# Second output projection in two groups of row tiles, and the first panel's products in another order, in a two-block transformer kernel

## The chip, the cores and the metric

The kernel runs on one core of a Trainium2 chip. The metric is the device time of one execution in microseconds; the median of three runs is taken.

## What is computed

Two transformer blocks follow each other on x of 1024 positions by 1024 features, all in f32. The stretches that matter here are the end of each block's mixer and the way into its feed-forward part:

```python
# first block
x_new = x + g1 * _merge(o_a, o_b, on_a[l], on_b[l], w_out[l])
h2 = _modulate(_rms_norm(x_new, norm2_g[l]), sh2, sc2)
x_new = x_new + g2 * _swiglu(h2, w_gate[l], w_up[l], w_down[l])
...
# second block
m = jnp.concatenate([a, b], axis=-1) @ w_out[l]
h = h + rmsnorm(m, post_mix_g[l])
f = rmsnorm(h, pre_ff_g[l]) @ w_ff1[l]
f = jnp.square(jax.nn.relu(f)) @ w_ff2[l]
h = h + rmsnorm(f, post_ff_g[l])
```

Here rmsnorm divides a row by the root of its mean square and multiplies by a gain. `w_out` is 1024 by 1024, `w_gate` and `w_up` 1024 by 2816, `w_ff1` 1024 by 4096.

## The kernel before

**Tiles.** The 1024 positions are eight row tiles of 128 (NT = 8). An f32 product is made of three products in a rounded format: each operand is split into a high part (a copy on ScalarE, ACT) and a low part (the difference, on VectorE, DVE), and TensorE (PE) adds hi by hi, lo by hi and hi by lo in one PSUM bank. A weight panel has 256 columns (PN); its split is one 128x2048 instruction on ACT (`split_hi`, L384) and one on DVE (`split_lo`, L388). A row tile's product with a panel is 24 matmuls (L403 to L405).

**The second output projection** is `leave_pe`, `leave_act`, `leave_dve`, `leave_pool` and `leave_sp`. It runs over 4 panels, and in each over the 8 row tiles. During panel 0 PE also turns (transposes) the next row of the operand (`turn_mixed`, L2874). ACT copies each finished tile from PSUM to `q_nat` (L2911), and in the last panel squares the row that is now whole, 1024 wide, and sums it (L2915). GpSimd (POOL) makes the row's root from the sum in two small operations (L2858, L2860). DVE then scales by root and gain (L2942) and adds to the residual `x_res` (L2946): two steps. ACT squares the new row (`square_row`, L1383), POOL makes its root (`root_row`, L1387 and L1389), and DVE scales it into `ff_rows` (`scale`, L2951). PE turns rows 0 to 3 as whole rows (`turn_row`, L1397), and ACT and DVE split them (L1416, L1420).

**The up projection** is made by `seven`, once for the first block (`f1`, names with swiglu) and once for the second (`f2`, names with ff). It takes 7 block products P1 to P7 for each pair of weight blocks (index q counts the pairs) where 8 would be usual, for which half rows and weight blocks are added and subtracted beforehand: on DVE `mix_first`, `mix_second`, `mix_third` (L1435 to L1448) for rows and `weight_sum` (L1500) for weights. The weights for a product are split by `weight_hi` (ACT, L1476) and `weight_lo` (DVE, L1480). A product (L1519 to L1521) is 12 matmuls of 512 columns.

**The first pair, q = 0,** needs the late rows turned, in five groups (g = 0 to 4) of four half rows (j = 0 to 3): `turn_block` on PE (L1411), then `block_hi` on ACT (L1424) and `block_lo` on DVE (L1428). `blocks_pe`, `blocks_act` and `blocks_dve` write the order of this stretch out by hand, the same for both blocks. On PE it is P1, P2, groups 0, 1 and 2, then P6, group 3, P5, group 4, P7, P3, P4. In the first block the same stretch follows its own output projection (`merge_*`), which already runs in 8 groups of 4 tiles (`OUT_PART`, `OUT_COL`, with columns 1 and 0 loaded twice) and interleaves the rows' additions (L2092), `modulate` (L2101, L2104) and row squares. Every engine does its own list in the order written; semaphores hold it where it needs another.

## Time and profile before

| | |
|---|---|
| three runs | 2496.49, 2500.88, 2500.69 us, median 2500.69 us |
| the profiled execution | 2507.9 us, its span 2505.7 us |
| mean granted clock of PE | 0.977 of full speed |
| PE busy, of the span | 2392.7 us, 95% |
| DVE busy | 1567.3 us, 63% |
| ACT busy | 1036.3 us, 41% |
| POOL busy | 258.0 us, 10% |

The span runs from the first to the last recorded instruction; what lies around it is 2.2 us in this execution. Busy shares are averages over stages that have different limits: PE's 5% of idle time lies in a few places, two of which are the stretches that the change touches. The profiled execution is 7 us above the median of the three runs, so differences are reckoned in the trace and laid on both.

### The profile page before, as it was taken

How to read it: one execution, taken by the hardware profiler on the slowest of the kernel's cores; microseconds unless marked ns; L12 is line 12 of the kernel's file. 1: busy time of each engine (PE TensorE's matmuls, PEld its weight loads, DVE VectorE, ACT ScalarE, POOL GpSimd, SP SyncE). 2: the span in 40 equal slices, each digit the busy share in tenths (PEclk: the TensorE clock that was granted, in tenths of full speed). 3: DMA queues.
4: the chain of work that ended last, by engine and by line, in shares of the span. 5: the costliest groups of instructions: out<-in, count | busy, mean ns of one | idle time of the engine just before them, and what ended most of it. 6: DMA issues, size and time to landing. Idle time of an engine off the chain costs nothing.

```text
span 2505.7 us, 40944 instructions
## 1 busy us (share of the span) xinstructions
PE 2392.7 (95%) x15691; PEld 2050.3 (82%) x15691; DVE 1567.3 (63%) x2612; ACT 1036.3 (41%) x1972; POOL 258.0 (10%) x253
## 2 busy tenths in 40 slices
PE   5799999999898999999999999999979999999998
PEld 2798888788797888888888898899968888788886
DVE  3632327778768777777668923234287777666677
ACT  1422226676523332332444432433255444444444
POOL 0566310000101000000000100012040000000002
PEclk8899999999998999999999999999989999999999
DMA  9233330000331232232666421110313444477553
GB/s 322 70 118 117 118 84 9 2 2 27 110 127 68 81 126 93 97 125 77 228 198 199 162 68 43 35 35 35 135 68 111 167 139 156 147 256 235 151 176 118
DMA packets 191115, 290.32 MB, mean 116 GB/s; under 512 B 11736, under 2 KB 112028, under 8 KB 190620
## 3 DMA queue, kind: packets, MB, share of 16 engines
q1 hardware_dynamic: 190940, 287.94, 34.7%
q8 instruction: 116, 1.90, 0.3%
q14 instruction: 59, 0.48, 0.1%
HBM read 221.56 MB, written 67.34 MB: 115 GB/s over the span
## 4 chain that ended last, share of the span: by engine, by line
PE 66%; DVE 3%; DMA 2%; issue 1%; POOL 1%; ACT 1%; SPq 0%; POOLq 0%; DVEq 0%; ACTq 0%
PE ps L1519 9%; PE ps L1520 9%; PE ps L1521 9%; PE ps L1761 6%; PE ps L1762 6%; PE ps L1763 6%; PE ps L403 4%; PE ps L404 4%; PE ps L405 4%; PE ps L1982 1%; PE ps L1984 1%; PE ps L1983 1%; PE ps L1411 1%; DMA stage<-w_out 0%; PE ps L2554 0%
## 5 line engine op out<-in xcount | busy, mean ns | idle before, releaser
L403 PE MATMUL ps<-w_hi,ht_hi 128*128 128x256 f32 x1488 | 435.3, 293 | 21.2 <-DVE w_lo L388 14.8
L404 PE MATMUL ps<-w_lo,ht_hi 128*128 128x256 f32 x1488 | 426.6, 287 | 0.0
L405 PE MATMUL ps<-w_hi,ht_lo 128*128 128x256 f32 x1488 | 426.3, 287 | 0.0
L403 PEld LDWEIGHTS ps<-w_hi,ht_hi 128*128 128x128 f32 x1488 | 290.9, 196 | 42.8 <-issue 20.1
L404 PEld LDWEIGHTS ps<-w_lo,ht_hi 128*128 128x128 f32 x1488 | 291.4, 196 | 0.5 <-issue 0.5
L405 PEld LDWEIGHTS ps<-w_hi,ht_lo 128*128 128x128 f32 x1488 | 291.1, 196 | 0.0
L1761 PE MATMUL ps<-ff_b_hi,ff_a_hi 128*128 128x512 f32 x448 | 174.5, 390 | 3.3 <-issue 2.1
L1763 PE MATMUL ps<-ff_b_hi,ff_a_lo 128*128 128x512 f32 x448 | 174.3, 389 | 0.0
L1762 PE MATMUL ps<-ff_b_lo,ff_a_hi 128*128 128x512 f32 x448 | 174.3, 389 | 0.0
L1519 PE MATMUL ps<-ht_hi,swiglu_w_hi 128*128 128x512 f32 x352 | 137.3, 390 | 2.4 <-DVE swiglu_gate L1558 2.4
L1722 ACT ACTIVATE ff_a_hi<-ff_a_raw 128x512 fp32r<-128x512 f32 x112 | 70.7, 631 | 165.9 <-PE ps L1763 148.8
L1520 PE MATMUL ps<-ht_lo,swiglu_w_hi 128*128 128x512 f32 x352 | 137.0, 389 | 0.0
L1521 PE MATMUL ps<-ht_hi,swiglu_w_lo 128*128 128x512 f32 x352 | 137.0, 389 | 0.0
L1476 ACT ACTIVATE swiglu_w_hi<-swiglu_stage 128x512 fp32r<-128x512 f32 x110 | 68.9, 630 | 161.7 <-PE ps L1521 153.3
L1747 DVE TENSOR_TENSOR ff_a_lo<-ff_a_raw,ff_a_hi 128x512 fp32r<-128x512 f32 x112 | 77.4, 691 | 90.0 <-ACT ff_a_hi L1722 89.8
L388 DVE TENSOR_TENSOR w_lo<-stage,w_hi 128x2048 fp32r<-128x2048 f32 x27 | 62.2, 2304 | 112.4 <-ACT w_hi L384 112.2
L1761 PE MATMUL ps<-swiglu_b_hi,swiglu_a_hi 128*128 128x512 f32 x308 | 120.7, 392 | 2.9 <-DVE swiglu_b_lo L1749 2.9
L1762 PE MATMUL ps<-swiglu_b_lo,swiglu_a_hi 128*128 128x512 f32 x308 | 120.2, 390 | 0.0
L1763 PE MATMUL ps<-swiglu_b_hi,swiglu_a_lo 128*128 128x512 f32 x308 | 120.1, 390 | 0.0
L852 ACT ACTIVATE probs<-masked,small 128x641 f32<-128x641 f32 (+3 forms) x128 | 112.0, 877 | 7.6 <-DVE small L939 5.8
L284 POOL TENSOR_SCALAR msq<-sumsq 128x1 f32<-128x1 f32 (+1 forms) x26 | 6.8, 262 | 1046.0 <-ACT junk L296 708.6
L1519 PE MATMUL ps<-ht_hi,ff_w_hi 128*128 128x512 f32 x256 | 100.8, 394 | 10.7 <-DVE ht_lo L1420 9.0
(371 smaller groups left out, 5792.0 us busy)
## 6 DMA issues: line engine op xcount, KB each, us to landing
ff_a_raw<-ff_act_dram SPq DMA_DIRECT2D x112, 256.0 KB, 2.8
stage<-w_in SPq DMA_DIRECT2D x23, 1024.0 KB, 5.3
swiglu_a_raw<-swiglu_act_dram SPq DMA_DIRECT2D x77, 256.0 KB, 2.9
stage<-w_mod SPq DMA_DIRECT2D x16, 1024.0 KB, 5.4
ff_stage<-w_ff SPq DMA_DIRECT2D x16, 1024.0 KB, 5.5
ff_act_dram<-ff_act_sums SPq DMA_DIRECT2D x16, 1024.0 KB, 4.3
ff_act_dram<-ff_acts SPq DMA_DIRECT2D x16, 768.0 KB, 5.8
swiglu_stage<-w_gate SPq DMA_DIRECT2D x11, 1024.0 KB, 6.3
```

The lines of the kernel that those rows point to most:

```text
L403: pe.matmul(bank, a, wh[:, k, :], start=(k == 0), stop=False)
L404: pe.matmul(bank, a, wl[:, k, :], start=False, stop=False)
L405: mm = pe.matmul(bank, b, wh[:, k, :], start=False, stop=(k == KT - 1))
L852: act.activation(probs_s[:, j, first:8 + CTX + width], masked_s[:, j, first:8 + CTX + width], ACT.Exp, bias=low, scale=-1.0, accum_out=den ...
L1519: pe.matmul(bank(q, b), w7_hi[b][:, k, :], x_of(0, b, k), start=(k == 0), stop=False)
L1520: pe.matmul(bank(q, b), w7_hi[b][:, k, :], x_of(1, b, k), start=False, stop=False)
L1521: mm = pe.matmul(bank(q, b), w7_lo[b][:, k, :], x_of(0, b, k), start=False, stop=(k == 3))
L1722: act.activation(a_hi[r][:, :], a_raw[s % LOOK][:, :], ACT.Copy).then_inc(f.a2_hi, 1)
L1747: dve.tensor_tensor(a_lo[r][:, :], a_raw[s % LOOK][:, :], a_hi[r][:, :].bitcast(F32), ALU.subtract).then_inc(f.a2_lo, 1)
L1761: pe.matmul(bank, a_hi[r][:, cols], b_hi[r][:, :], start=first, stop=False)
L1762: pe.matmul(bank, a_hi[r][:, cols], b_lo[r][:, :], start=False, stop=False)
L1763: return pe.matmul(bank, a_lo[r][:, cols], b_hi[r][:, :], start=False, stop=last)
```

## The change

It has two parts.

**The second output projection** takes the form of the first block's. The tiles run in 8 groups of 4 over six panel loads: rows 0 to 3 through panels 0 to 3, then rows 4 to 7 through columns 2, 3, 1 and 0; columns 1 and 0 are loaded and split a second time. ACT no longer copies a tile: it squares it straight from PSUM (`square`, after.py L2974) into a partial sum `o_sq`, 256 wide. DVE takes the tile out of PSUM with a multiplication by the gain (`evict`). POOL adds four partial sums in two small operations before the two it had (`mixed_root`). DVE adds to the residual in one step (`add`, a multiplication by the root and an addition). Whole rows 0 to 3 are turned after tiles (4, 3), (5, 0), (5, 2) and (6, 0) of the new count.

**The first pair's products** in both blocks run in the order P1, P2, P3, P5, P7, P6, P4, each placed before the last half row (or the last two) of a group; the groups have another order too (1 is now the first half of rows 0 to 3, 2 the first half and 3 the mixed second half of rows 4 to 7), and the products' PSUM banks another. P3's weights, which are made from the last weight sum, now come third on ACT and DVE. The last two `mix_first` stand inside `blocks_dve`, and the wait for the stored rows (`x1_stored`, `x3_stored`) stands behind the keeping of P1.

The diff, cut to its core:

```diff
         P1, P2, P6, P5, P7, P3, P4 = range(7)
+        FIRST = (P1, P2, P3, P5, P7, P6, P4)
...
-                    pe.wait_ge(f.mixed, f0.mixed + (8 + j + 1, 2 * j + 1, 2 * j + 2, 12 + j + 1)[g - 1])
-                pe.wait_ge(f.lo7, f0.lo7 + (3 + j // 2 if g == 0 else e + 1))
-                source = (half(4 + j, 1), half(4 + j, 1), half(j, 0), half(4 + j, 0), half(j, 1))[g]
+                    pe.wait_ge(f.mixed, f0.mixed + (2 * j + 1, 2 * j + 2, 8 + j + 1, 12 + j + 1)[g - 1])
+                held = [x for x in range(e) if late_at(x) == late_at(e)]
...
             def bank(q, b):
+                if q == 0:
+                    return ps[:, (0, 1, 7, 3, 0, 2, 4)[b], :]
                 return ps[:, (7 * q + b) % 4, :]
...
-                    pe.wait_ge(f.lo7, f0.lo7 + {P1: 4, P2: 4, P6: 12, P5: 16, P7: 20, P3: 8, P4: 24}[b])
-                if 7 * q + b >= 4:
+                    pe.wait_ge(f.lo7, f0.lo7 + {P1: 4, P2: 4, P3: 8, P5: 12, P7: 16, P6: 20, P4: 24}[b])
+                    if b == P7:
...
             f.turn_block(pe, 0, 3)
-            for g in (1, 2):
-                for j in range(4):
-                    f.turn_block(pe, g, j)
+            for j in range(3):
+                f.turn_block(pe, 1, j)
             pe.wait_ge(dense_evac, evac)
+            f.product(pe, 0, P3)
+            f.turn_block(pe, 1, 3)
+            for j in range(3):
+                f.turn_block(pe, 2, j)
+            f.product(pe, 0, P5)
+            f.turn_block(pe, 2, 3)
+            for j in range(3):
+                f.turn_block(pe, 3, j)
+            f.product(pe, 0, P7)
+            f.turn_block(pe, 3, 3)
+            f.turn_block(pe, 4, 0)
+            f.turn_block(pe, 4, 1)
             f.product(pe, 0, P6)
-            for j in range(4):
-                f.turn_block(pe, 3, j)
-            f.product(pe, 0, P5)
-            for j in range(4):
-                f.turn_block(pe, 4, j)
-            for b in (P7, P3, P4):
-                f.product(pe, 0, b)
+            f.turn_block(pe, 4, 2)
+            f.turn_block(pe, 4, 3)
+            f.product(pe, 0, P4)
             for q in range(1, f.Q):
                 for b in range(7):
                     f.product(pe, q, b)
 
-        def blocks_act(act, f):
+        def blocks_act(act, f, stored):
 
             for g in range(2):
                 for j in range(4):
                     f.block_hi(act, g, j)
-            for b in (P7, P3, P4):
+            for b in (P7, P6, P4):
                 f.weight_hi(act, 0, b)
             f.tick_act(act, 0, P1)
+            act.wait_ge(*stored)
+            for j in range(4):
+                f.block_hi(act, 2, j)
             f.tick_act(act, 0, P2)
...
+            f.mix_first(dve, 2)
             for j in range(4):
-                f.mix_second(dve, j)
                 f.block_lo(dve, 0, j)
+            f.mix_first(dve, 3)
             for j in range(4):
-                f.mix_third(dve, j)
                 f.block_lo(dve, 1, j)
-            for b in (P7, P3, P4):
-                f.weight_lo(dve, 0, b)
-            for g in (2, 3, 4):
-                for j in range(4):
-                    f.block_lo(dve, g, j)
+            f.weight_lo(dve, 0, P7)
+            for j in range(4):
+                f.block_lo(dve, 2, j)
+            f.mix_second(dve, 0)
+            f.mix_second(dve, 1)
+            f.block_lo(dve, 3, 0)
+            f.mix_second(dve, 2)
+            f.block_lo(dve, 3, 1)
+            f.mix_second(dve, 3)
+            f.block_lo(dve, 3, 2)
+            f.weight_lo(dve, 0, P6)
+            f.mix_third(dve, 0)
+            f.block_lo(dve, 3, 3)
+            f.mix_third(dve, 1)
+            f.block_lo(dve, 4, 0)
+            f.mix_third(dve, 2)
+            f.block_lo(dve, 4, 1)
+            f.mix_third(dve, 3)
+            f.weight_lo(dve, 0, P4)
+            f.block_lo(dve, 4, 2)
+            f.block_lo(dve, 4, 3)
...
-            for b in (P1, P2, P6, P5):
+            for b in (P1, P2, P3, P5):
                 f1.weight_hi(act, 0, b)
                 if b == P2:
                     square(4)
             for j in range(5, NT):
                 square(j)
             act.wait_ge(dense_done, OUT_END)
-            act.wait_ge(x1_stored, 16 * NT)
-            blocks_act(act, f1)
+            blocks_act(act, f1, (x1_stored, 16 * NT))
 
...
+            load_weights(sp, P_M + 2, panel_of(t["w_out_2"], OUT_COL[2] * PN))
             sp.wait_ge(tr_done, T_M + NT)
-            for j in range(NT):
-                sp.dma_start(x_res[:, j, :], x2_dram[j * P:(j + 1) * P, :]).then_inc(x_in[j], 16)
-            for p in range(2, 4):
-                load_weights(sp, P_M + p, panel_of(t["w_out_2"], p * PN))
+            for j in range(4):
+                x2_row(j)
+            load_weights(sp, P_M + 3, panel_of(t["w_out_2"], OUT_COL[3] * PN))
+            for j in range(4, NT):
+                x2_row(j)
+            sp.dma_start(stage_x[:, :].rearrange("p (k n) -> p k n", k=KT), panel_of(t["w_out_2"], OUT_COL[5] * PN)).then_inc(w_landed_2, 16)
...
         def leave_pool(pool):
-            for j in range(NT + 2):
-                if j < NT:
-                    pool.wait_ge(m_sq, j + 1)
-                    pool.tensor_scalar(msq[:, 8 + j:9 + j], sumsq[:, 8 + j:9 + j], 1.0 / D, EPS, ALU.mult, ALU.add).then_inc(m_ms, 1)
-                    pool.wait_ge(m_ms, j + 1)
-                    pool.tensor_tensor(rstd[:, 8 + j:9 + j], msq[:, 8 + j:9 + j], neg_half[:, 8 + j:9 + j], ALU.pow).then_inc(m_rs, 1)
-                if j >= 2:
-                    f2.root_row(pool, j - 2)
+            def mixed_root(j):
+                pool.wait_ge(m_sq, all_parts(j))
+                pool.tensor_tensor(o_ms[:, j, 0:2], o_sq[:, j, 0:2], o_sq[:, j, 2:4], ALU.add).then_inc(m_ms, 1)
+                pool.wait_ge(m_ms, 3 * j + 1)
+                pool.tensor_tensor(sumsq[:, 8 + j:9 + j], o_ms[:, j, 0:1], o_ms[:, j, 1:2], ALU.add).then_inc(m_ms, 1)
+                pool.wait_ge(m_ms, 3 * j + 2)
+                pool.tensor_scalar(msq[:, 8 + j:9 + j], sumsq[:, 8 + j:9 + j], 1.0 / D, EPS, ALU.mult, ALU.add).then_inc(m_ms, 1)
+                pool.wait_ge(m_ms, 3 * j + 3)
+                pool.tensor_tensor(rstd[:, 8 + j:9 + j], msq[:, 8 + j:9 + j], neg_half[:, 8 + j:9 + j], ALU.pow).then_inc(m_rs, 1)
+
+            for first in (0, 4):
+                mixed_root(first)
+                for j in range(first, first + 3):
+                    mixed_root(j + 1)
+                    f2.root_row(pool, j)
+                f2.root_row(pool, first + 3)
...
-            f2.turn_row(pe, 3)
+            for h in range(8):
+                for i in range(4):
+                    mixed_tile(h, i)
+                    if (h, i) in OUT_TURN:
+                        turn_mixed(OUT_TURN[h, i])
+                    if (h, i) in MIX_ROW:
+                        f2.turn_row(pe, MIX_ROW[h, i])
...
+            def added_square(j):
+                act.wait_ge(added, j + 1)
+                act.wait_ge(m_sq, (18, 19, 20, 20, 30, 31, 32, 32)[j])
+                f2.square_row(act, j, x_res[:, j, :])
...
-                        act.wait_ge(added, j - 1)
-                        act.wait_ge(m_sq, min(j + 1, NT))
-                        f2.square_row(act, j - 2, x_res[:, j - 2, :])
-                    if p == 3 and LAG_M <= j < LAG_M + 4:
-                        act.wait_ge(dense_done, D_M + 3 * NT + j - LAG_M + 1)
-                        f2.row_hi(act, j - LAG_M)
+            split(1)
+            for h in range(7):
+                for i in range(4):
+                    if (h, i) in OUT_TURN:
+                        j = OUT_TURN[h, i]
+                        turned_hi(act, j, j % 2, T_M)
+                    square(h, i)
+                    if (h, i) in MIX_SPLIT:
+                        split(MIX_SPLIT[h, i])
+                    if h == 4 and i:
+                        added_square(i - 1)
...
+            def evict(h, i):
+                x, first = OUT_PART[h]
+                j, cols = first + i, slice(OUT_COL[x] * PN, (OUT_COL[x] + 1) * PN)
+                dve.wait_ge(m_sq, 4 * h + i + 1)
...
+                    dve.wait_ge(tr_done, T_M + NT)
...
             def add(k):
                 dve.wait_ge(m_rs, k + 1)
-                dve.scalar_tensor_tensor(out=q_nat[:, k, :], in0=q_nat[:, k, :], scalar=rstd[:, 8 + k:9 + k], in1=gain_m[:, :],
-                                         op0=ALU.mult, op1=ALU.mult).then_inc(m_scaled, 1)
-                dve.wait_ge(m_scaled, k + 1)
+                dve.wait_ge(dense_evac, D_M + all_parts(k))
                 dve.wait_ge(x_in[k], 48)
-                dve.tensor_tensor(x_res[:, k, :], x_res[:, k, :], q_nat[:, k, :], ALU.add).then_inc(added, 1)
+                dve.scalar_tensor_tensor(out=x_res[:, k, :], in0=q_nat[:, k, :], scalar=rstd[:, 8 + k:9 + k], in1=x_res[:, k, :],
+                                         op0=ALU.mult, op1=ALU.add).then_inc(added, 1)
...
+            add(0)
+            evict(4, 0)
+            add(1)
+            add(2)
+            evict(4, 1)
+            add(3)
+            evict(4, 2)
+            scale(0)
+            evict(4, 3)
```

Three places of the order, each word for word. The first is POOL in the second output projection: L2858 and L2860 make the root of the projection's row, L1387 and L1389 that of the new residual row. Before, from the root of the projection's row 2 on:

```order
L2858 TENSOR_SCALAR msq<-sumsq 128x1
L2860 TENSOR_TENSOR rstd<-msq,neg_half 128x1
L1387 TENSOR_SCALAR ff_means<-ff_sums 128x1
L1389 TENSOR_TENSOR ff_roots<-ff_means,neg_half 128x1
L2858 TENSOR_SCALAR msq<-sumsq 128x1
L2860 TENSOR_TENSOR rstd<-msq,neg_half 128x1
L1387 TENSOR_SCALAR ff_means<-ff_sums 128x1
L1389 TENSOR_TENSOR ff_roots<-ff_means,neg_half 128x1
```

After, where L2913 to L2919 are `mixed_root` and L1397 and L1399 `root_row`; the fence begins with the root of row 1:

```order
L2913 TENSOR_TENSOR o_ms<-o_sq 128x2
L2915 TENSOR_TENSOR sumsq<-o_ms 128x1
L2917 TENSOR_SCALAR msq<-sumsq 128x1
L2919 TENSOR_TENSOR rstd<-msq,neg_half 128x1
L1397 TENSOR_SCALAR ff_means<-ff_sums 128x1
L1399 TENSOR_TENSOR ff_roots<-ff_means,neg_half 128x1
L2913 TENSOR_TENSOR o_ms<-o_sq 128x2
L2915 TENSOR_TENSOR sumsq<-o_ms 128x1
L2917 TENSOR_SCALAR msq<-sumsq 128x1
L2919 TENSOR_TENSOR rstd<-msq,neg_half 128x1
```

A row takes four POOL operations where it took two, and the roots of residual row 0 stand between the mixed roots of rows 1 and 2 (before, between those of rows 2 and 3).

The second place is ACT at the end of the first block's output projection: L1476 is `weight_hi`, `swiglu_stage_8608` the loaded weights, `swiglu_w_s` a weight sum, L1383 the square of a residual row. Before:

```order
L1476 ACTIVATE swiglu_w_hi_8610<-swiglu_stage_8608 128x512
L1476 ACTIVATE swiglu_w_hi_8611<-swiglu_stage_8608 128x512
L1383 ACTIVATE junk,swiglu_sums<-q_nat 128x1024
L1476 ACTIVATE swiglu_w_hi_8612<-swiglu_w_s_8625 128x512
L1476 ACTIVATE swiglu_w_hi_8613<-swiglu_w_s_8624 128x512
L1383 ACTIVATE junk,swiglu_sums<-q_nat 128x1024 x3
```

After, with L1487 for `weight_hi` and L1393 for the row square:

```order
L1487 ACTIVATE swiglu_w_hi_8610<-swiglu_stage_8608 128x512
L1487 ACTIVATE swiglu_w_hi_8611<-swiglu_stage_8608 128x512
L1393 ACTIVATE junk,swiglu_sums<-q_nat 128x1024
L1487 ACTIVATE swiglu_w_hi_8612<-swiglu_stage_8608 128x512
L1487 ACTIVATE swiglu_w_hi_8613<-swiglu_w_s_8624 128x512
L1393 ACTIVATE junk,swiglu_sums<-q_nat 128x1024 x3
```

The third weight split reads `swiglu_stage_8608` in place of the sum `swiglu_w_s_8625`; what it reads there is the block that `weight_sum` 3 writes in place, and row 5's square stands behind it.

The third place is PE in the second block's first pair, from the last matmul of P2 to the first ones of the next products: L1411 is the turning of half rows, x4 for each half row. Before:

```order
L1521 MATMUL ps<-ht_hi,ff_w_lo_8757 128x512
L1411 MATMUL ps<-ident,ff_rows 128x128 x40
L1519 MATMUL ps<-ff_t_hi_8741,ff_w_hi_8751 128x512
L1520 MATMUL ps<-ff_t_lo_8744,ff_w_hi_8751 128x512
L1521 MATMUL ps<-ff_t_hi_8741,ff_w_lo_8758 128x512
```

After, with L1422 for the turning and L1536 to L1538 for products:

```order
L1538 MATMUL ps<-ht_hi,ff_w_lo_8757 128x512
L1422 MATMUL ps<-ident,ff_rows 128x128 x20
L1536 MATMUL ps<-ht_hi,ff_w_hi_8751 128x512
L1537 MATMUL ps<-ht_lo,ff_w_hi_8751 128x512
L1538 MATMUL ps<-ht_hi,ff_w_lo_8758 128x512
```

Forty turnings, ten half rows, stood between P2 and the next product; now it is twenty, five half rows, and the next product is P3, which reads operands of group 0's kind (`ht_hi`) where P6 read those of group 1 (`ff_t_hi_8741`).

## Rows read from the trace of the kernel before

**Rows 1.** Page, part 1: busy time, share of the span, instructions

```profile
PE 2392.7 (95%) x15691; PEld 2050.3 (82%) x15691; DVE 1567.3 (63%) x2612; ACT 1036.3 (41%) x1972; POOL 258.0 (10%) x253
```

**Rows 2.** Waits of PE: line, released by; us in total, times, longest

```profile
PE ps L1519 <- DVE ht_lo L1420: 9.0, 1, 9.0
...
PE ps L1411 <- DVE ht_lo L1428: 4.2, 3, 3.3
```

**Rows 3.** Timeline of PE: start, duration, line; idle time before it in brackets

```profile
816.79 0.47 PE L1519 MATMUL ps<-ht_hi,swiglu_w_hi 128*128 128x512 f32 x1 [1.33 <-DVE swiglu_gate L1558]
...
835.95 0.39 PE L1519 MATMUL ps<-ht_hi,swiglu_w_hi 128*128 128x512 f32 x1
...
1740.88 0.36 PE L403 MATMUL ps<-w_hi,ht_hi 128*128 128x256 f32 x1 [1.76 <-DVE ht_lo L2932]
...
1744.62 0.36 PE L403 MATMUL ps<-w_hi,ht_hi 128*128 128x256 f32 x1
...
1843.96 0.28 PE L404 MATMUL ps<-w_lo,ht_hi 128*128 128x256 f32 x1
1844.08 0.28 PE L405 MATMUL ps<-w_hi,ht_lo 128*128 128x256 f32 x1
...
1862.29 0.77 PE L1519 MATMUL ps<-ht_hi,ff_w_hi 128*128 128x512 f32 x1 [8.95 <-DVE ht_lo L1420]
```

**Rows 4.** Timeline of DVE, the first panels of both blocks

```profile
781.61 1.22 DVE L2104 TENSOR_TENSOR swiglu_rows<-swiglu_rows,mod 128x1024 f32<-128x1024 f32 x1
...
800.83 2.48 DVE L1428 TENSOR_TENSOR swiglu_t_lo<-ps,swiglu_t_hi 128x512 fp32r<-128x512 f32 x4 [1.53 <-ACT swiglu_t_hi L1424]
805.31 2.48 DVE L1428 TENSOR_TENSOR swiglu_t_lo<-ps,swiglu_t_hi 128x512 fp32r<-128x512 f32 x4 [2.00 <-ACT swiglu_t_hi L1424]
...
1866.10 1.28 DVE L2951 SCALAR_TENSOR_TENSOR ff_rows<-x_res,ff_roots,gain_g 128x1024 f32<-128x1024 f32 x1
...
1885.16 2.48 DVE L1428 TENSOR_TENSOR ff_t_lo<-ps,ff_t_hi 128x512 fp32r<-128x512 f32 x4 [2.46 <-ACT ff_t_hi L1424]
1889.65 2.48 DVE L1428 TENSOR_TENSOR ff_t_lo<-ps,ff_t_hi 128x512 fp32r<-128x512 f32 x4 [2.00 <-ACT ff_t_hi L1424]
```

**Rows 5.** Groups by shape, 1740:1900 (L2088: 700:810): busy us, mean ns, idle before

```profile
L2911 ACT ACTIVATE q_nat<-ps 128x256 f32<-128x256 f32 x32 | 11.9, 382 | 36.9 <-PE ps L405 36.6
...
L1428 DVE TENSOR_TENSOR ff_t_lo<-ps,ff_t_hi 128x512 fp32r<-128x512 f32 x12 | 7.7, 683 | 4.5 <-ACT ff_t_hi L1424 4.5
...
L388 DVE TENSOR_TENSOR w_lo<-stage,w_hi 128x2048 fp32r<-128x2048 f32 x3 | 6.9, 2288 | 27.7 <-ACT w_hi L384 27.7
...
L2088 DVE TENSOR_TENSOR tmp<-ps,mod 128x256 f32<-128x256 f32 x24 | 10.1, 422 | 21.8 <-PE ps L1984 21.8
```

**Rows 6.** Timeline of all engines, 766.9 to 769.4, two rows

```profile
767.00 1.06 ACT L1383 ACTIVATE junk<-q_nat 128x1024 bf16<-128x1024 f32 x1 [0.69 <-DVE q_nat L2092]
...
769.34 0.68 DVE L1500 TENSOR_TENSOR swiglu_stage<-swiglu_stage,swiglu_w_s 128x512 f32<-128x512 f32 x1
```

**Rows 7.** Windows: length, busy of PE, PEld, DVE, ACT, POOL; granted clock, DMA

```profile
794.00:796.00 2.00, 1.85 (x9) 1.51 (x9) 2.00 (x4) 2.00 (x5) 0.00 (x0) 0.50 0.00 0
...
798.00:800.00 2.00, 2.00 (x13) 1.65 (x12) 1.29 (x3) 0.00 (x0) 0.00 (x0) 1.00 0.95 264
```

**Rows 8.** Timelines of the DMA queue and of ACT, second output projection

```profile
1763.59 3.71 SPq L2844 DMA_DIRECT2D x_res<-x_dram  x8
1768.19 16.76 SPq L235 DMA_DIRECT2D stage<-w_out  x2
...
1780.30 1.91 ACT L384 ACTIVATE w_hi<-stage 128x2048 fp32r<-128x2048 f32 x1 [10.57 <-DMA stage<-w_out]
```

**Rows 9.** Timeline of POOL, last panel of the second output projection

```profile
1823.48 0.19 POOL L2858 TENSOR_SCALAR msq<-sumsq 128x1 f32<-128x1 f32 x1 [84.72 <-ACT junk L2915]
1823.75 0.56 POOL L2860 TENSOR_TENSOR rstd<-msq,neg_half 128x1 f32<-128x1 f32 x1
...
1831.12 1.29 POOL L1387 TENSOR_SCALAR ff_means<-ff_sums 128x1 f32<-128x1 f32 x1
```

243 lines of the change are left out of this document (165 added, 78 removed).

## The prediction

> **What bounds the kernel now.** I read the page's first part for where idle time can be, then the chain of waits of PE, then the timelines of PE, DVE, ACT and POOL round the two stretches that the change touches. PE is busy 95% of 2505.7 us [rows 1], so the kernel is PE's work plus some pauses. Pauses that count here: 9.0 us at once before the second block's first product, and 4.2 us at turnings that wait for DVE's low parts [rows 2]. But PE's own pauses do not say what ends the stretch. In both first panels DVE is the slow one. Its last scaled row starts at 781.61 and ends at 782.83, and the low parts of the last half rows end at 805.31 + 2.48 = 807.79: 24.96 us. In the second block it is 1866.10 + 1.28 = 1867.38 to 1889.65 + 2.48 = 1892.13: 24.75 us [rows 4]. Only 1.53 + 2.00 us (first) and 2.46 + 2.00 us (second) of them is idle. The first product of q = 1 starts 9.0 us after DVE's last low part, at 816.79 [rows 3]. From there PE runs through. So each stretch is priced by when DVE hands over its last low part.
>
> **First block, rows.** In the new order P3's weights are split third. They read the block that weight sum 3 writes, which DVE does at 769.34 for 0.68 us, so ACT can't begin before 770.0. Before, row 5's square ran at 767.00 [rows 6]; now it is queued behind two weight splits on ACT, from about 771.1, and row 5's root on POOL, `modulate(5)` on DVE and all that DVE does after it wait for it. With a square of 1.06 us and 0.19 for reading its sum, a root of 0.82 us (0.19 + 0.08 + 0.55, [rows 9]) and DVE's own work up to there I get row 5 ready at 773.6 where DVE was free at 771.9: **+1.7**. What hides it otherwise is nothing: DVE has no pause from there to the last row. It would be 0 if DVE came later than I think, 3 at most (POOL's two operations at 1.29 each instead of 0.19 and 0.55 when DVE is in the way).
>
> **Both blocks, the first panel.** From the last scaled row, DVE has the same work in another order: 35 instructions of 128x512, at 0.60 us from one to the next (four take 2.48, one alone 0.68 [rows 4, 5], so the step is 1.80/3), 21.0 us, and 0.4 us of pauses between dependent ones: 21.4. The rest is idle. Before that was 3.5. In the new order DVE waits more often, since PE turns the last half row of every group behind a product: 1.3 us for half row (1, 3), behind P3; 2.0 for group 2, because ACT has three weight splits, the keeping of P1 and a wait ahead of it; 1.2 for group 3 behind P5; 1.65 for its last half row behind P7; 1.35 for the last two behind P6. Each comes out of laying the four lists side by side with the durations of the rows: a product is (835.95 - 816.79)/7 = 2.74 us at full clock [rows 3], four turnings 0.43 (a turning of eight is 0.86, below), a half row on ACT about as long as on DVE. Sum 7.5, so the stretch is 21.4 + 7.5 = 28.9 against 24.96 (first) and 24.75 (second): **+3.9 and +4.1**. The move of the two `mix_first` and of the wait for stored rows costs nothing by itself: they are in the 35, and the stores are long done. From below this could be -3.5 each (no idle at all, 21.4); from above +8 each (every product at half clock stands before a half row that DVE needs).
>
> **The clock.** Between 794 and 796 PE has nothing but turnings, is busy 1.85 of 2 us and is granted 0.50, the 1.2 GHz level; between 798 and 800, with products, it has 1.00 [rows 7]. In the new order products stand between turnings from the start, each while the clock is still at the lower level. P3 then takes 5.5 us in place of 2.74, P5 perhaps part of it, and DVE waits for the half row behind them. On DVE's path I put one such product and half of a second one, less the time that DVE had work in hand: **+4** in each block, between 0 and 8.
>
> **Second output projection.** PE's plain work: the first tile starts at 1740.88; a tile is 24 matmuls at 0.12 us (1843.96 to 1844.08) = 2.88, and with eight turnings 1744.62 - 1740.88 = 3.74, so eight turnings are 0.86 [rows 3]. Thirty-two tiles and ten turnings of eight (six of the operand, four rows of `ff_rows`) end at 1740.88 + 92.2 + 8.6 = 1841.7. To this come:
> - Panel 3. The eight rows of x_res were issued at 1763.59 ahead of the panels at 1768.19, and the panel's split began at 1780.30, after ACT had waited 10.57 for it [rows 8]. Now panel 3 is behind four rows and panel 2; by the same rate (5.2 MB in 16.7 us) it lands at 1777.9 and, with 1.91 on ACT [rows 8] and 2.29 on DVE [rows 5], is split at 1782.3. Tile (3, 0) would start at 1740.88 + 34.6 + 5.2 = 1780.7: **+1.6**.
> - Row 0. POOL's roots of mixed row 2 stand behind the roots of residual row 0, which wait for ACT's square of it, behind tile (4, 1) in ACT's list. So: tile (4, 1) done 1799.6, its square 0.57 (0.38 as the eviction of the same shape [rows 5] and 0.19), row square 1.25, POOL root 0.82, mixed root 1.36 (two more operations of 0.27), and the same again for row 1's root and mixed row 3, with DVE's additions of 1.28 [rows 4] and evictions of 0.42 (as L2088, [rows 5]) between. DVE has `add(2)` before tile (4, 1)'s eviction and `add(3)` before (4, 2)'s: `add(3)` ends at 1808.8, `scale(0)` at 1810.4 or so. PE reaches the turning of row 0 after tile (4, 3) at 1805.3: **+5.2**. Row 2 then waits 0.8, and the clock falls once more behind the pause, 1.4.
>
> That gives 1841.7 + 1.6 + 5.2 + 0.8 + 1.4 = 1850.7 for the end of the tiles, against 1844.2 now. It is not lost whole: of rows 4 to 7 less is left to do behind the tiles (one addition step of 1.28 where there were 1.28 and 1.22, and no square of 1024 behind a copy), so the last row is scaled 15.5 us behind the tiles in place of 1867.38 - 1844.2 = 23.2: 1866.2 against 1867.4, **-1.1**. The 9.0 us wait before the first product [rows 2, 3] goes into this. From below this part could be -8 (row 0 in time, POOL free), from above +4: POOL's small operations take 1.29 where one of DVE's is under way, as at 1831.12, in place of 0.19 [rows 9], and there are now two more for a row.
>
> **Sum.** First block 1.7 + 3.9 + 4 = 9.6, second -1.1 + 4.1 + 4 = 7.0: +16.6. The profiled execution of before is 2507.9, so 2524.5 there; on the median, 2500.69 + 16.6 = **2517**. The same layout for the kernel before ends within 0.7 us of its rows, so it is the new waits that can be wrong.
>
> **Rivals.**
> - *The clock doesn't matter.* If PE comes back to full clock with P3, the 8 and the 1.4 fall away: +7.2, 2507.9. For it: products stand closer together than before. Against it: at 794 to 796 it had stayed low through 1.85 us of work in 2. 0.16. The Trainium skill (TensorE: Matmul & The Clock Gate, Part 4: PE-mode transpose) says that a transpose doesn't count as PE being busy in the same way; by that rule products between turnings would bring the clock back sooner, which is this rival, and the trace agrees as far as the clock rose only with products.
> - *No change.* The clock is up and also row 0 is in time, because tile (4, 1)'s square is served at once and POOL isn't slowed: 7.2 - 5.2 = +2.0, 2502.7. 0.11.
> - *Faster.* DVE never waits in the two first panels, as the products' order means to have it: first block 1.7 + 21.4 - 24.96 = -1.9, second -1.1 + 21.4 - 24.75 = -4.5, together -6.4: 2494.3. What decides is DVE's idle time in a stretch: with x us in each, the sum is -6.4 + 2x, so below 3.2 us the kernel gains, and I count 7.5. For it: the new order gives DVE half rows of four groups to choose from. Against it: DVE's list is fixed, and the last half row of each group is behind a product of 2.74. 0.12.
> - *Worse.* Panel 3 comes later than the rate says (the first panels' loads share the queue) and the clock is low through three products in each block: 2517 + 9 or more. 0.05.
>
> The main case has the rest, 0.56, between 2506 and 2526 by its own bounds.
>
> **Range and chances.** 0.2%, 5 us, is about what a measurement can tell from no change, so "slower" begins at 2505.7. Slower: the main case, most of the first rival and the last, 0.71; the same 0.17; faster 0.12. The range takes in the main case, the clock rival and most of the next: 2501 to 2527.
>
> **What would show it.** PE waits some 5 us at a row's turning for `ff_rows` of the second block and 1 to 2 us for the low part of panel 3; the half-row stretch on DVE lasts 28 us or more with 7 or more idle, in five pieces; row 5's `modulate` in the first block waits for POOL; q = 1 starts in the first block at 822 to 827 where it was 816.79; the granted clock is 0.50 at P3. I am wrong if DVE's idle time stays under 3 us in the stretches, or if row 0's turning doesn't wait.

## The result and the profile after

| | before | after |
|---|---|---|
| median | 2500.78 us (4 runs, 2496.49 to 2505.99) | 2521.22 us (4 runs, 2518.58 to 2527.16) |
| ratio | | 1.0076, 95% interval 1.0055 to 1.0098 |
| profiled execution, its span | 2507.9, 2505.7 us | 2518.58, 2516.8 us |

The kernel is slower by 20.4 us. The two profiled executions lie only 10.7 us apart: the first block's output projection began at 664.05 before and at 658.84 after, in a part that the change doesn't touch. So positions are compared from a start of their own: in the first block from the first matmul of the output projection, in the second from the first tile of the projection there. The page after:

```profile
span 2516.8 us, 41059 instructions
...
PE 2393.7 (95%) x15691; PEld 2052.8 (82%) x15691; DVE 1575.2 (63%) x2638; ACT 1036.1 (41%) x1990; POOL 252.0 (10%) x269
```

PE's busy time is what it was (2392.7, [rows 1]). Its waits, answering to [rows 2]; L1536 is the first line of a product, L1422 the turning of a half row, L1407 of a whole row:

```profile
PE ps L1536 <- DVE swiglu_gate L1575: 5.9, 1, 5.9
PE ps L1422 <- DVE ff_rows L3069: 5.6, 2, 3.3
PE ps L1536 <- DVE ff_acts L1575: 5.2, 1, 5.2
...
PE ps L1407 <- DVE ff_rows L3069: 4.9, 2, 4.5
...
PE ps L2952 <- DVE w_lo L388: 1.5, 1, 1.5
```

The 9.0 us before P1 of the second block is gone, and the same time and more stands in many places: 5.9 and 5.2 us before q = 1 of each block, 4.9 at the turning of whole rows, 1.5 for panel 3. Now the timeline of PE, answering to [rows 3]:

```profile
820.44 0.76 PE L1536 MATMUL ps<-ht_hi,swiglu_w_hi 128*128 128x512 f32 x1 [5.87 <-DVE swiglu_gate L1575]
...
842.45 0.39 PE L1536 MATMUL ps<-ht_hi,swiglu_w_hi 128*128 128x512 f32 x1
...
1746.03 0.36 PE L2952 MATMUL ps<-w_hi,ht_hi 128*128 128x256 f32 x1 [1.67 <-issue]
...
1787.50 0.39 PE L2952 MATMUL ps<-w_hi,ht_hi 128*128 128x256 f32 x1 [1.52 <-DVE w_lo L388]
...
1815.29 1.97 PE L1407 MATMUL ps<-ident,ff_rows 128*128 128x128 f32 x8 [4.50 <-DVE ff_rows L3069]
...
1855.91 0.28 PE L2954 MATMUL ps<-w_hi,ht_lo 128*128 128x256 f32 x1
```

The tiles of the second projection issue from 1746.03 to 1855.91, 109.9 us (before 103.2). The seven products of q = 1 in the first block take 842.45 - 820.44 = 22.0 us where they took 835.95 - 816.79 = 19.2 [rows 3]. DVE in the first block's half-row stretch, answering to [rows 4]: the last scaled row, and the half rows before which it sat idle most.

```profile
777.41 1.22 DVE L2146 TENSOR_TENSOR swiglu_rows<-swiglu_rows,mod 128x1024 f32<-128x1024 f32 x1
...
788.39 0.69 DVE L1439 TENSOR_TENSOR ht_lo<-ps,ht_hi 128x512 fp32r<-128x512 f32 x1 [2.92 <-ACT ht_hi L1435]
...
791.45 2.56 DVE L1439 TENSOR_TENSOR swiglu_t_lo<-ps,swiglu_t_hi 128x512 fp32r<-128x512 f32 x4 [1.76 <-ACT swiglu_t_hi L1435]
...
795.98 0.69 DVE L1439 TENSOR_TENSOR swiglu_t_lo<-ps,swiglu_t_hi 128x512 fp32r<-128x512 f32 x1 [0.78 <-ACT swiglu_t_hi L1435]
...
799.10 0.69 DVE L1439 TENSOR_TENSOR swiglu_t_lo<-ps,swiglu_t_hi 128x512 fp32r<-128x512 f32 x1 [0.64 <-ACT swiglu_t_hi L1435]
...
804.31 0.69 DVE L1439 TENSOR_TENSOR swiglu_t_lo<-ps,swiglu_t_hi 128x512 fp32r<-128x512 f32 x1 [3.31 <-ACT swiglu_t_hi L1435]
...
810.16 1.29 DVE L1439 TENSOR_TENSOR swiglu_t_lo<-ps,swiglu_t_hi 128x512 fp32r<-128x512 f32 x2 [1.30 <-ACT swiglu_t_hi L1435]
```

From 777.41 + 1.22 = 778.63 to 810.16 + 1.29 = 811.45 it is 32.8 us in place of 24.96, with 10.9 us idle in place of 3.5. The same in the second block, from the last scaled row to the last half rows, with the wait behind P7 between them:

```profile
1870.03 1.28 DVE L3069 SCALAR_TENSOR_TENSOR ff_rows<-x_res,ff_roots,gain_g 128x1024 f32<-128x1024 f32 x1 [0.94 <-POOL ff_roots L1399]
...
1894.29 0.69 DVE L1439 TENSOR_TENSOR ff_t_lo<-ps,ff_t_hi 128x512 fp32r<-128x512 f32 x1 [2.35 <-ACT ff_t_hi L1435]
...
1900.13 1.29 DVE L1439 TENSOR_TENSOR ff_t_lo<-ps,ff_t_hi 128x512 fp32r<-128x512 f32 x2 [1.29 <-ACT ff_t_hi L1435]
```

That is 30.1 us (24.75), with 8.1 idle. The granted clock (window, its length, busy PE, PEld, DVE, ACT, POOL, clock, DMA), answering to [rows 7]:

```profile
784.00:786.00 2.00, 2.00 (x7) 1.52 (x7) 1.47 (x3) 0.14 (x1) 0.00 (x0) 0.61 0.00 0
786.00:788.00 2.00, 2.00 (x15) 1.74 (x13) 0.00 (x0) 0.24 (x1) 0.00 (x0) 1.00 0.00 0
800.00:802.00 2.00, 2.00 (x6) 1.59 (x5) 0.99 (x2) 0.00 (x0) 0.00 (x0) 0.50 0.00 0
822.00:824.00 2.00, 2.00 (x7) 1.51 (x6) 1.29 (x3) 0.79 (x2) 0.00 (x0) 0.50 0.00 0
1876.00:1878.00 2.00, 2.00 (x10) 1.60 (x9) 2.00 (x4) 0.00 (x0) 0.00 (x0) 1.00 0.00 0
```

In the first block P3, issued from 783.15 on, begins at the lower level and ends at full clock: the mean is 0.61 from 784 to 786 and 1.00 from 786 to 788. P7, at 800 to 802, is at 0.50, and so is P1 of q = 1 at 822 to 824. In the second block P3 is at full clock (1876 to 1878).

**Where the time went**, from such rows of both traces: in the first block, 1.3 us until the last row (from row 4's scaling at 766.88 and 761.38), 7.9 in the stretch, 2.8 in q = 1: 12.0. In the second, the last row is scaled 125.3 us after the first tile, before 126.5: -1.2; the stretch +5.4; q = 1 +2.7: 6.9. Together 18.9, inside the interval of the ratio (13.8 to 24.5 us). The two spans differ by only 11.1 us because the stretches that the change doesn't touch took 7.4 us less in the profiled execution of after, 5.2 of it ahead of the first block's output projection.

### The profile page after: what moved, and what is told of

It reads as the page before. It is cut to its first block and busy times, and to the rows that moved or that the text cites. A ratio compares the mean times of both kernels' runs of the same rounds, so it can differ in the third digit from the quotient of the medians.

```text
span 2516.8 us, 41059 instructions
## 1 busy us (share of the span) xinstructions
PE 2393.7 (95%) x15691; PEld 2052.8 (82%) x15691; DVE 1575.2 (63%) x2638; ACT 1036.1 (41%) x1990; POOL 252.0 (10%) x269
## 5 line engine op out<-in xcount | busy, mean ns | idle before, releaser
L403 PE MATMUL ps<-w_hi,ht_hi 128*128 128x256 f32 x1232 | 361.6, 293 | 17.6 <-DVE w_lo L388 14.8
L404 PE MATMUL ps<-w_lo,ht_hi 128*128 128x256 f32 x1232 | 353.6, 287 | 0.0
L405 PE MATMUL ps<-w_hi,ht_lo 128*128 128x256 f32 x1232 | 353.6, 287 | 0.0
L403 PEld LDWEIGHTS ps<-w_hi,ht_hi 128*128 128x128 f32 x1232 | 241.4, 196 | 38.8 <-issue 16.0
L404 PEld LDWEIGHTS ps<-w_lo,ht_hi 128*128 128x128 f32 x1232 | 241.8, 196 | 0.5 <-issue 0.5
L405 PEld LDWEIGHTS ps<-w_hi,ht_lo 128*128 128x128 f32 x1232 | 241.4, 196 | 0.0
L1536 PE MATMUL ps<-ht_hi,swiglu_w_hi 128*128 128x512 f32 x352 | 139.1, 395 | 6.1 <-DVE swiglu_gate L1575 5.9
L1538 PE MATMUL ps<-ht_hi,swiglu_w_lo 128*128 128x512 f32 x352 | 138.2, 393 | 0.0
L1487 ACT ACTIVATE swiglu_w_hi<-swiglu_stage 128x512 fp32r<-128x512 f32 x110 | 69.2, 630 | 166.8 <-PE ps L1538 153.7
L852 ACT ACTIVATE probs<-masked,small 128x641 f32<-128x641 f32 (+3 forms) x128 | 112.0, 877 | 7.6 <-DVE small L939 5.8
L788 PE MATMUL ps<-ident,probs 128*128 128x128 f32 (+1 forms) x720 | 106.6, 283 | 1.0 <-DVE prob_t L947 1.0
```

Source lines behind the costliest of these rows:

```text
L403: pe.matmul(bank, a, wh[:, k, :], start=(k == 0), stop=False)
L404: pe.matmul(bank, a, wl[:, k, :], start=False, stop=False)
L405: mm = pe.matmul(bank, b, wh[:, k, :], start=False, stop=(k == KT - 1))
L788: mm = pe.transpose(ps[0:rows, 4 + c // 4, (c % 4) * P:(c % 4 + 1) * P], probs[:, j, c * P:c * P + rows], ident[:, :])
L852: act.activation(probs_s[:, j, first:8 + CTX + width], masked_s[:, j, first:8 + CTX + width], ACT.Exp, bias=low, scale=-1.0, accum_out=den ...
L1536: pe.matmul(bank(q, b), w7_hi[w_at(q, b)][:, k, :], x_of(0, b, k), start=(k == 0), stop=False)
```

## Experiments

Twelve kernels. The table has each run's ratio to before on the same chip, and from its trace: *stretch*, from the end of the last scaled row to the end of the last half row's low part, and the idle time of DVE in it; *q = 1*, from its first product to the first of q = 2; *tiles*, from the first to the last matmul of the second projection; *row*, from that first tile to the end of the last scaled row. All in us.

| kernel | ratio (95%) | block 1 stretch, idle, q = 1 | tiles, row | block 2 stretch, idle, q = 1 |
|---|---|---|---|---|
| before | 1 | 25.0, 3.5, 19.2 | 103.2, 126.5 | 24.8, 4.5, 19.1 |
| after | 1.0076 (1.0055 to 1.0098) | 32.8, 10.9, 22.0 | 109.9, 125.3 | 30.1, 8.1, 21.8 |
| leave_only | 0.9994 (0.9982 to 1.0006) | 24.4, 2.9, 19.1 | 109.5, 124.9 | 25.5, 4.1, 19.1 |
| order_only | 1.0093 (1.0074 to 1.0113) | 31.9, 10.0, 21.8 | 104.1, 125.9 | 35.2, 13.0, 20.6 |
| leave_pool | 0.9973 (0.9962 to 0.9984) | 25.5, 4.1, 19.2 | 103.2, 118.6 | 24.5, 3.0, 19.1 |
| after_pool | 1.0051 (1.0034 to 1.0068) | 32.4, 10.5, 21.9 | 103.2, 118.6 | 29.9, 8.0, 21.8 |
| whole_groups | 1.0041 (1.0025 to 1.0056) | 26.1, 4.4, 21.7 | 109.5, 124.9 | 26.6, 4.9, 21.8 |
| act_group2 | 1.0089 (1.0073 to 1.0105) | 32.1, 10.2, 21.7 | 112.3, 127.7 | 30.6, 8.7, 21.9 |
| row5_first | 1.0082 (1.0065 to 1.0099) | 32.1, 10.2, 21.9 | 109.9, 125.3 | 30.1, 8.1, 21.7 |
| pool_fill | 0.9950 (0.9937 to 0.9963) | 23.9, 0.0, 19.0 | 104.9, 120.3 | 24.7, 0.8, 19.0 |
| pool_fill_sp | 0.9945 (0.9932 to 0.9958) | 25.8, 2.0, 19.0 | 101.4, 116.8 | 25.3, 1.4, 19.0 |
| new_repaired | 1.0000 (0.9991 to 1.0010) | 28.3, 6.6, 21.3 | 101.4, 116.8 | 25.1, 3.4, 21.3 |
| pause_filled | 1.0061 (1.0044 to 1.0078) | 32.4, 10.4, 19.2 | 112.0, 127.4 | 30.2, 8.2, 19.1 |
| turns_filled | 0.9932 (0.9915 to 0.9949) | 24.1, 0.4, 19.0 | 101.4, 116.8 | 24.1, 0.4, 19.0 |

### One part alone

**leave_only**: the change without its part on the first pair's order.

```diff
-            for b in (P1, P2, P3, P5):
+            for b in (P1, P2, P6, P5):
                 f2.weight_hi(act, 0, b)
...
             scale(7)
+            f2.mix_first(dve, 2)
+            f2.mix_first(dve, 3)
             blocks_dve(dve, f2)
```

> The second output projection in its new form, the first pair's products in the order of before. My theory: the projection itself neither gains nor loses. Its tiles end about 6.5 us later than before (some 1.5 us for the low part of panel 3, some 4.5 us at the turning of row 0), but the last scaled row comes about 1 us earlier relative to the first tile, and the half-row stretch on DVE is again 24 to 25 us. Time within 0.2% of before, 2496 to 2506 us; the first block as before. Rival: the pauses of PE in the projection are the loss, then this kernel keeps 6 to 10 us of the 20, and the stretch of the first block is not where it goes.

Measured 2501.65 us, ratio 0.9994: no change, as the theory had it, with the tiles 6.3 us longer and the last row 1.6 us earlier.

**order_only**: the other part alone, on the old projection (`blocks_*`, `seven` and `first_weights_*` of after, `leave_*` of before).

> The projection of before, the new order of the first pair's products in both blocks. My theory: this is the whole loss. In the first block q = 2 starts 11 to 12 us later after the first tile of its output projection than before, the half-row stretch on DVE is 32 to 33 us with some 11 us idle; in the second block the stretch is 29 to 31 us with 7 to 8 us idle. Sum 17 to 21 us over before, 2518 to 2522 us. Rival: the loss is in the projection, then this kernel is within 8 us of before.

Measured 2526.72 us, ratio 1.0093: 22.6 us, a little over the 17 to 21 expected, and the rival is out: the order is the whole loss. The second block's stretch is 35.2 us where 29 to 31 were expected, with 13.0 idle. 4.2 us of that is in a place where the changed kernel has none, ahead of group 0's half rows on DVE:

```profile
1880.53 1.29 DVE L1439 TENSOR_TENSOR ht_lo<-ps,ht_hi 128x512 fp32r<-128x512 f32 x2 [1.92 <-ACT ht_hi L1435]
1884.09 1.29 DVE L1439 TENSOR_TENSOR ht_lo<-ps,ht_hi 128x512 fp32r<-128x512 f32 x2 [2.27 <-ACT ht_hi L1435]
```

Behind the old projection's 9 us wait P1 is issued from 1873.72 on, 3.6 us ahead of the last scaled row's end, where the changed kernel has it 15.3 us ahead. It takes 5.25 us at a granted clock of 0.50, and group 0's half rows are turned behind it and behind P2. In before P1 is nearly as late, 5.1 us ahead, but there DVE has the mixing of half rows between the same low parts.

### POOL's order

**leave_pool** and **after_pool**: leave_only and the changed kernel with the roots in this order.

```diff
-            for first in (0, 4):
-                mixed_root(first)
-                for j in range(first, first + 3):
-                    mixed_root(j + 1)
-                    f2.root_row(pool, j)
-                f2.root_row(pool, first + 3)
+            for j in range(4):
+                mixed_root(j)
+            for j in range(4):
+                f2.root_row(pool, j)
+            mixed_root(4)
+            for j in range(4, 7):
+                mixed_root(j + 1)
+                f2.root_row(pool, j)
+            f2.root_row(pool, 7)
```

> As leave_only, with one further edit: GpSimd makes the roots of mixed rows 0 to 3 first and those of residual rows 0 to 3 behind them, so that mixed row 2 is not queued behind residual row 0. My theory: the 4.5 us wait of PE at the turning of row 0 goes (under 1 us stays), the tiles end 5 us earlier, the clock does not fall behind it, and the last scaled row comes with them: 5 to 8 us less than leave_only, 2493 to 2497 us. Rival: DVE's own list (additions and evictions) or ACT's squares hold row 0 just as long, then the wait stays above 3 us and the time is that of leave_only within 2 us.

> The changed kernel with that edit of GpSimd's order alone. My theory: the same 5 to 8 us less than the changed kernel, 2513 to 2516 us, the rest of the loss stays. Rival: in this kernel the last row hangs on DVE, not on the tiles, and nothing is gained.

The wait first, in the changed kernel: POOL's timeline where mixed row 2's four operations (L2913 on) stand behind the root of residual row 0 (L1397, L1399), and DVE's, where L3061 is the one-step addition, first of row 1 and then of row 2.

```profile
1806.87 0.19 POOL L1397 TENSOR_SCALAR ff_means<-ff_sums 128x1 f32<-128x1 f32 x1 [11.38 <-ACT junk L1393]
1807.15 0.55 POOL L1399 TENSOR_TENSOR ff_roots<-ff_means,neg_half 128x1 f32<-128x1 f32 x1
1807.66 0.19 POOL L2913 TENSOR_TENSOR o_ms<-o_sq 128x2 f32<-128x2 f32 x1
```

```profile
1803.04 1.28 DVE L3061 SCALAR_TENSOR_TENSOR x_res<-q_nat,rstd,x_res 128x1024 f32<-128x1024 f32 x1
1809.08 1.28 DVE L3061 SCALAR_TENSOR_TENSOR x_res<-q_nat,rstd,x_res 128x1024 f32<-128x1024 f32 x1 [4.76 <-POOL rstd L2919]
...
1813.96 1.27 DVE L3069 SCALAR_TENSOR_TENSOR ff_rows<-x_res,ff_roots,gain_g 128x1024 f32<-128x1024 f32 x1
```

POOL sat idle for 11.38 us before the root, and DVE for 4.76 us before row 2's addition; row 0's scaling (L3069) ran at 1813.96 and PE, ready for it since 1810.8, began to turn it at 1815.29. In leave_pool, PE's turning of the whole row 0 (L1397) has no wait:

```profile
1804.00 1.04 PE L1397 MATMUL ps<-ident,ff_rows 128*128 128x128 f32 x8
```

The tiles are back to 103.2 us and the last row comes at 118.6: 2496.51 us, ratio 0.9973, and 2515.24, 1.0051, for after_pool. Both as forecast; the gains over the kernels without the edit are 5 and 6 us.

### Inside the half-row stretch

**whole_groups**: the changed kernel with products behind whole groups on PE.

```diff
-            for j in range(3):
+            for j in range(4):
                 f.turn_block(pe, 1, j)
             pe.wait_ge(dense_evac, evac)
             f.product(pe, 0, P3)
-            f.turn_block(pe, 1, 3)
-            for j in range(3):
+            for j in range(4):
                 f.turn_block(pe, 2, j)
...
```

> The changed kernel with the new order of products, but on PE each product stands behind the whole of a group: four half rows of group 1, P3, group 2, P5, group 3, P7, group 4, P6, P4. My theory: DVE's idle time in the first block's half-row stretch (10.9 us in the changed kernel) is for 7.5 us that of half rows turned behind a product (2.92 behind P3, 3.31 behind P7, 1.30 behind P6). These pieces go, at most a third comes back elsewhere: 3 to 6 us idle, stretch 25.5 to 28.5 us in place of 32.8, 4 to 7 us in the first block and 3 to 5 in the second, 2509 to 2514 us. Rival: DVE waits for the banks and for its own mixing (the half rows are turned as soon as they can be), then the idle time stays above 9 us and the time within 3 us.

Measured 2512.37 us, ratio 1.0041, 8 to 9 us less than the changed kernel. DVE's timeline in the first block:

```profile
793.26 2.48 DVE L1439 TENSOR_TENSOR swiglu_t_lo<-ps,swiglu_t_hi 128x512 fp32r<-128x512 f32 x4 [1.95 <-ACT swiglu_t_hi L1435]
...
797.73 0.69 DVE L1439 TENSOR_TENSOR swiglu_t_lo<-ps,swiglu_t_hi 128x512 fp32r<-128x512 f32 x1 [0.78 <-ACT swiglu_t_hi L1435]
...
804.79 0.69 DVE L1439 TENSOR_TENSOR swiglu_t_lo<-ps,swiglu_t_hi 128x512 fp32r<-128x512 f32 x1 [1.31 <-ACT swiglu_t_hi L1435]
```

The idle time fell from 10.9 to 4.4 us and the stretch from 32.8 to 26.1, in the second block from 8.1 to 4.9 and from 30.1 to 26.6: what had cost was the half row left behind a product. In the first block P7 ran at full clock this time, so some 2 of the 6.7 us there can be the clock's. In the second it took 4.4 us, for the most part at the lower level, and the idle time fell all the same. But q = 1 still takes 21.7 us: that part of the loss has another cause.

**act_group2**: ScalarE's copies of group 2 ahead of two weight splits and of the keeping of P1 (`block_hi(act, 2, j)` behind `weight_hi(act, 0, P7)`).

> The changed kernel with ScalarE's copies of group 2 ahead of two of the three weight splits and of the keeping of P1. My theory: DVE's idle time before group 2 (1.76 us in both blocks) goes, the weight split of P6 is in time as before, 1 to 2 us less in each stretch, 2 to 4 us in all. Rival: group 2 is late on PE, behind P3 and its turnings, then nothing changes (within 1 us in the traces).

Measured 2524.81 us, ratio 1.0089, no gain. DVE's timeline:

```profile
792.47 1.88 DVE L1439 TENSOR_TENSOR swiglu_t_lo<-ps,swiglu_t_hi 128x512 fp32r<-128x512 f32 x3
796.21 0.69 DVE L1439 TENSOR_TENSOR swiglu_t_lo<-ps,swiglu_t_hi 128x512 fp32r<-128x512 f32 x1 [1.86 <-ACT swiglu_t_hi L1435]
...
799.26 0.69 DVE L1439 TENSOR_TENSOR swiglu_t_lo<-ps,swiglu_t_hi 128x512 fp32r<-128x512 f32 x1 [1.16 <-ACT swiglu_t_hi L1435]
```

Three half rows of group 2 are now taken at 792.47 without a pause, and the fourth waits 1.86 us at 796.21: it is turned behind P5, and was so in the changed kernel too. The pause had two causes in a row, and taking away the first showed the second: from the end of (1, 3)'s low part to the end of the stretch it is 22.3 us, and 22.4 in the changed kernel. So ScalarE's list did hold group 2, as the theory said, but it was not worth the 1 to 2 us. The rival's forecast, nothing gained, came true, with another product than the one it named: P5, not P3.

**row5_first**: the square of row 5 ahead of the third weight split.

```diff
             for b in (P1, P2, P3, P5):
                 f1.weight_hi(act, 0, b)
                 if b == P2:
                     square(4)
-            for j in range(5, NT):
+                    square(5)
+            for j in range(6, NT):
                 square(j)
```

> The changed kernel with the square of row 5 ahead of the third weight split in the first block on ScalarE. My theory: the last scaled row of the first block comes 1 to 1.7 us earlier relative to its projection's first tile (119.8 to 121.2 us in the runs with the new order, 117.9 to 120.2 in those with the old one), the stretch behind it is as long as it was: 1 to 2 us. Rival: P3's low part is then late and DVE waits for it in the place of the row: no difference.

Measured 2522.66 us, ratio 1.0082: no difference that the times can tell. The trace of the changed kernel shows what there was to get, on DVE:

```profile
761.38 1.28 DVE L2143 SCALAR_TENSOR_TENSOR swiglu_rows<-q_nat,swiglu_roots,mod 128x1024 f32<-128x1024 f32 x1
...
765.22 0.69 DVE L1491 TENSOR_TENSOR swiglu_w_lo<-swiglu_stage,swiglu_w_hi 128x512 fp32r<-128x512 f32 x1 [0.70 <-ACT swiglu_w_hi L1487]
...
767.74 1.28 DVE L2143 SCALAR_TENSOR_TENSOR swiglu_rows<-q_nat,swiglu_roots,mod 128x1024 f32<-128x1024 f32 x1 [0.43 <-POOL swiglu_roots L1399]
```

0.70 us is the way from sum 3 over ScalarE to P3's low part, only 0.43 us is row 5's root. In row5_first the wait for the root went and the 0.70 stayed: from row 4's scaling to the last row 16.7 us, where the changed kernel has 17.25 and before 15.95.

### The pause before q = 1, and the clock

**pause_filled**: the changed kernel with work of no use in PE's pause.

```diff
             f.product(pe, 0, P4)
+            for i in range(24):
+                pe.matmul(ps[:, 5, :], ht_hi[:, 0, 0:P], ht_hi[:, 0, 0:512], start=True, stop=True)
```

> The changed kernel with 24 more matmuls of 512 columns on PE, behind P4 of the first pair and ahead of q = 1, into a PSUM bank that nobody reads: some 5.5 us of work in a pause of 5.2 to 5.9 us. The result is not touched. My theory: PE's late pause costs nothing itself, since q = 1 starts when DVE is done; what costs is that the clock is at its lower level for some 5 us behind it. Filled, q = 1 starts within 0.5 us of where it did, at full clock, and the seven products of q = 1 take 19.1 us in place of 21.8 to 22.0: 2.7 us in each block, 5 us in all, 2514 to 2518 us. Rival: the products of q = 1 are slow since they wait for weights or for joined banks, then they take 21.8 us again, at full clock.

Measured 2520.09 us, ratio 1.0061. PE's timeline and a window of the first products of q = 1 (L1907 is the filling):

```profile
816.43 5.60 PE L1907 MATMUL ps<-ht_hi 128*128 128x512 f32 x24
822.47 0.47 PE L1536 MATMUL ps<-ht_hi,swiglu_w_hi 128*128 128x512 f32 x1 [0.44 <-DVE swiglu_gate L1575]
```

```profile
824.00:826.00 2.00, 2.00 (x11) 1.63 (x10) 1.33 (x3) 1.31 (x3) 0.00 (x0) 1.00 0.00 0
```

q = 1 takes 19.2 and 19.1 us in the two blocks, at 1.00, and starts 0.44 us behind the filling. So the 2.8 us there is the clock alone: it is down behind PE's pause of 5.9 us, and the pause itself costs nothing, as q = 1 waits for DVE anyway. This holds for the trace. The time missed the 2514 to 2518 us that I expected, and the 5 us are not shown by it: ratio 1.0061 against the changed kernel's 1.0076, with intervals that overlap. In this profiled run the second projection's tiles took 2 us more (112.0).

### Towards a faster kernel

**pool_fill**: leave_pool with work of q = 1 in DVE's two pauses of the old order.

```diff
             for g in (2, 3, 4):
                 for j in range(4):
                     f.block_lo(dve, g, j)
+                if g < 4:
+                    f.weight_lo(dve, 1, (P1, P2)[g - 2])
+                    f.weight_sum(dve, 1, g - 2)
+            f.join(dve, 0, 0)
             for q in range(f.Q):
                 for b in range(7):
-                    f.tick_dve(dve, q, b)
+                    if q or b not in (P1, P2):
+                        f.tick_dve(dve, q, b)
```

> From the version with the new projection, the old order of products and GpSimd's roots reordered: the low parts of the next pair's first two weights and its first two sums are done on DVE in its two pauses before groups 3 and 4, in place of behind group 4. My theory: the 9 us from the last low part of the half rows to the first product of q = 1 become some 7 us, the pauses of PE before P7 and q = 1 (about 1.1 and 0.7 us) go, and up to 1 us more per block: 2 to 4 us in all, 2492 to 2495 us where the version it comes from had 2496.5. Rival: group 3 and 4 are pushed back by the same amount because the pauses (1.5 and 2.0 us) are not where I put the work, and nothing is gained.

Measured 2491.0 us, ratio 0.9950.

```profile
798.35 0.68 DVE L1480 TENSOR_TENSOR swiglu_w_lo<-swiglu_stage,swiglu_w_hi 128x512 fp32r<-128x512 f32 x1
798.95 0.68 DVE L1500 TENSOR_TENSOR swiglu_w_s<-swiglu_stage 128x512 f32<-128x512 f32 x1
799.55 2.48 DVE L1428 TENSOR_TENSOR swiglu_t_lo<-ps,swiglu_t_hi 128x512 fp32r<-128x512 f32 x4
```

The weight's low part (L1480) and the sum (L1500) lie where the pause was, and group 3 begins behind them without waiting. From DVE's last low part to q = 1 it is 6.3 us in both blocks, where it was 9.0 and 8.3. The time is below the 2492 to 2495 us expected.

**pool_fill_sp**: with it, `load_weights(sp, P_M + 3, ...)` ahead of all residual rows in `leave_sp`, and so also ahead of the wait for the operand's last turning (`tr_done`) that stands before them.

> As pool_fill, with the load of the projection's panel 3 issued ahead of the residual rows in place of behind four of them. My theory: the 1.5 to 1.8 us wait of PE for the low part of panel 3 at tile (3, 0) goes and the tiles end 1.5 to 3 us earlier; the rows still come in time for the first addition. Time 1 to 3 us less than pool_fill. Rival: the low part waits for DVE's and ACT's own lists, not for the load; then the wait stays over 1 us.

Measured 2489.57 us, ratio 0.9945. In the trace the wait for panel 3's low part is gone and the tiles take 101.4 us, 1.8 us less than in leave_pool; the times don't tell it from pool_fill. Which of the two, the rows or the wait, had held the load was not separated.

**new_repaired**: whole_groups, row5_first, POOL's order and the early load together, to give the new order its best case.

> The changed kernel with the new order of products, repaired as far as the runs showed: products behind whole groups, row 5's square first, GpSimd's mixed roots first, panel 3's load first. My theory: the new order then still loses to the old one, by what PE's late pause before q = 1 (5 us, with the clock at its lower level behind it) and one to two us of DVE's stretch cost in each block: 2501 to 2507 us, 4 to 9 us over leave_pool (2496.5). Rival: the repairs make the two orders equal, 2494 to 2498 us.

Measured 2502.49 us, as forecast, ratio 1.0000 (0.9991 to 1.0010). It has all of the projection's gain, and the new order eats it: DVE's stretch is 28.3 us in the first block, and q = 1 takes 21.3 us in both.

**turns_filled**: pool_fill_sp with the clock kept up through the turnings.

```diff
-            for g in (1, 2):
-                for j in range(4):
-                    f.turn_block(pe, g, j)
             pe.wait_ge(dense_evac, evac)
+            for i in range(12):
+                pe.matmul(ps[:, 3, :], ht_hi[:, 0, 0:P], ht_hi[:, 0, 0:512], start=True, stop=True)
+            for g in (1, 2):
+                for j in range(4):
+                    f.turn_block(pe, g, j)
+                    pe.matmul(ps[:, 3, :], ht_hi[:, 0, 0:P], ht_hi[:, 0, 0:512], start=True, stop=True)
```

> The fastest version so far (pool_fill_sp) with 12 such matmuls ahead of group 1's turnings, where PE waits some 3 us, and one behind each half row's turning of groups 1 and 2. The result is not touched. My theory: the clock stays at full through the turnings or is back before P6, P6 takes 2.7 us in place of up to 5, group 3 is turned earlier and DVE's remaining pauses (2.0 and 1.4 us) go: 1 to 3 us less than pool_fill_sp. Rival: the extra matmuls stand in the way of turnings that DVE waits for, 1 to 4 us more.

Measured 2484.91 us, ratio 0.9932 (0.9915 to 0.9949), the lowest median of all, 18.0 us under before. Its interval overlaps pool_fill_sp's (0.9932 to 0.9958), so the gain over that kernel, 1 to 3 us expected and 4.7 between the medians, is likely but not shown by the times. P6 (L1519), directly behind the turnings, on PE:

```profile
790.94 0.63 PE L1411 MATMUL ps<-ident,swiglu_rows 128*128 128x128 f32 x4 [0.34 <-DVE swiglu_t_lo L1428]
791.33 0.47 PE L1876 MATMUL ps<-ht_hi 128*128 128x512 f32 x1
791.64 0.39 PE L1519 MATMUL ps<-swiglu_t_hi,swiglu_w_hi 128*128 128x512 f32 x1
...
792.34 0.39 PE L1519 MATMUL ps<-swiglu_t_hi,swiglu_w_hi 128*128 128x512 f32 x1
```

A window among the same turnings in turns_filled and, in the fence behind it, in pool_fill_sp:

```profile
788.00:790.00 2.00, 1.32 (x9) 0.87 (x9) 2.00 (x4) 2.00 (x5) 0.00 (x0) 1.00 0.00 0
```

```profile
790.00:792.00 2.00, 1.79 (x8) 1.03 (x7) 2.00 (x5) 0.80 (x3) 0.00 (x0) 0.50 0.00 0
```

The granted clock is 1.00 where it was 0.50, three matmuls of P6 take 0.70 us from 791.64 to 792.34, and DVE's idle time is 0.4 us in each stretch. That the fillings' matmuls cost PE time is hidden: PE waits for DVE there in both kernels.

## Why the prediction was right, and where not

The time was forecast at 2517 and measured at 2521.22 us. Of the 18.9 us in the traces 13.4 came from mechanisms that the prediction names, though not each at its size, and 5.5 from one that it leaves out. Its signs held: PE waited 4.5 us at row 0's turning and 1.5 us for panel 3, both stretches lasted over 28 us with over 7 idle, row 5's `modulate` waited for POOL, and the clock was at the lower level at P3's start in the first block, but not in the second. The start of q = 1, expected at 822 to 827, was at 820.44 in an execution that was 5.2 us ahead by the output projection's first matmul.

**The second projection** came out as laid side by side. The tiles' end was put at 1850.7 for a first tile at 1740.88, 109.8 us; measured 109.9. The wait at row 0's turning was 5.2, measured 4.50; panel 3's 1.6, measured 1.5; the last row -1.1, measured -1.2. That the tiles' end is so near has some luck in it. The row waits, 6.0 in sum, were 4.9 (4.50 and 0.40), and what is left of 109.9 behind 100.8 of plain work and 6.4 of waits, 2.7, is where I had 1.4 for the clock, which was at 0.50 from 1815 to 1817. And by the prediction's own rate panel 3's 4.2 MB land at 1777.0, not 1777.9, which would have made its wait 0.7. That POOL's list causes row 0's wait is shown by leave_pool, which takes the whole of it away with an edit of that list alone.

**Rows in the first block**, +1.7: measured +1.3, but of two terms. I had only row 5's root (0.43 us in the trace), not DVE's own wait for P3's high part (0.70), which the split of a weight made by a sum brings with it.

**The stretch.** I had 3.9 and 4.1 for the order and 4 for the clock in each, 7.9 and 8.1 in sum; measured +7.9 in the first block and +5.4 in the second. The pieces of idle time were 1.3, 2.0, 1.2, 1.65 and 1.35; measured in the first block 2.92, 1.76, 0.78 + 0.64, 3.31 and 0.18 + 1.30. The two large ones are those with P3 and P7 at the lower clock: I had put such a product at P3 and part of P5, and the clock was back by P5 and down again at P7. In the second block P3 ran at full clock, and its piece was 1.14: the clock's share at P3 was 1.8. At P7 the wait follows the product's length, from its first matmul to the next turning: 3.31 us for 4.95, 3.04 for 4.69 (order_only), 2.76 for 4.40 (act_group2), 2.35 for 3.99 (second block), each time 1.64 or 1.65 less. At full clock, 2.82 as P5 had, it would be 1.2, an estimate from these rows, so the clock's share there is 2.1 in the first block and 1.1 in the second. So the clock cost 3.9 in the first stretch, where I had 4, and only 1.1 in the second, where I also had 4: that is the term that was mis-sized. The 2.0 for ScalarE's list was there, 1.76, but behind it stood P5, as act_group2 shows.

**What I left out** is q = 1. The prediction has PE running through from the start of q = 1, as it did before. I had its start 9.0 us behind DVE's last low part, and it is (820.44 against 811.45). But only P4 is left behind group 4 now, where P7, P3 and P4 were, so PE ends the first pair earlier, stands for 5.9 us and comes back at half the rate: 2.8 and 2.7 us, which pause_filled takes away. The term called clock was 8 in all and belongs to two places. The errors in the second block's stretch (-2.7) and here (+5.5) partly cancel, so that the sum is nearer than its parts. That is luck.

**The rivals.** The clock one is out, though half of what it says is so. Products between turnings do bring the clock back: from P3's second half it is at 1.00, through sixteen turnings and P5. But it was down again for P7, behind waits of PE of 2.01 and 1.41 us with eight turnings between them, and down again behind the pause before q = 1. The faster one needed under 3.2 us idle; the stretches had 10.9 and 8.1.

Two things stay open. In order_only's second block 4.2 of the 4.9 us of added idle time lie behind P1 and P2; how much of it is P1's late place and how much its clock, no run separates. And the tiles' time of one form varies between profiled runs, from 109.5 to 112.3 us. In the two runs above 112 the clock was down behind the wait for panel 3 too, which was 1.85 us there (0.50 from 1787.5 to 1790.5 in pause_filled; in after 1.52 us, and 1.00 from 1787.5 to 1789.5); no run was made to fix it.

## What to carry to other kernels

Where the end of a stretch is set by one engine that follows its own list, write down for each item what the others' lists hold ahead of it; a product placed before the last item of a group made the next engine wait for it, and an engine's order of small operations (POOL's here) can be worth as much as the arithmetic that was saved. When one cause of a pause is removed, look for what stands next behind it before pricing it. A pause on TensorE that costs nothing itself can be paid behind it, at half the rate, as the 2.7 us in each block here. Filling it took that away in the trace, though the times of pause_filled don't show the gain; giving the other engine's work an earlier place (pool_fill) took away the old order's pauses there, 1.3 and 0.7 us, in a kernel whose median is 5.5 us lower.

## What the runs showed of the hardware

Turnings alone left the clock at its lower level, to which it had fallen in the waits ahead of them (0.50 at 790 to 792 in pool_fill_sp, PE busy 1.79 of 2 us); with twelve matmuls of 512 columns ahead and one behind each four turnings it was back and stayed at 1.00 (788 to 790 in turns_filled, PE busy only 1.32 of 2 us). Behind PE's pause of 5.87 us the first product of q = 1 ran at 0.50; behind one of 0.44 us it ran at 1.00. POOL's small operation took 0.19 us in most places, and up to 1.29 in the last panel of before [rows 9]; I had expected that this might hurt `mixed_root` with its two further operations. In after the four operations of a row took 1.4 us for rows 0 to 3, where DVE had little to do, and those of rows 4 to 7 took 2.2 to 3.3 us, while DVE ran operations of its own on rows and weights. One of them is the root of row 6:

```profile
1856.79 1.47 POOL L2919 TENSOR_TENSOR rstd<-msq,neg_half 128x1 f32<-128x1 f32 x1
```

The last scaled row still came within 0.1 us of its forecast.
